# Cross attention of a two-block transformer in pairs of heads: narrower query weight tiles and a new order of its steps among the matrix tiles

## What is computed

```python
def memory_cross_attention(h, mem_n, wq, wk, wv, wo):     # X_HEADS = 4, X_HEAD_DIM = 128
    q = (h @ wq).reshape(b, s, X_HEADS, X_HEAD_DIM)        # 256x2048 @ 2048x512
    k = (mem_n @ wk).reshape(b, m, X_HEADS, X_HEAD_DIM)
    v = (mem_n @ wv).reshape(b, m, X_HEADS, X_HEAD_DIM)
    sc = jnp.einsum('bshd,bmhd->bhsm', q, k).astype(jnp.float32) * (X_HEAD_DIM ** -0.5)
    p = jax.nn.softmax(sc, axis=-1).astype(v.dtype)
    o = jnp.einsum('bhsm,bmhd->bshd', p, v).reshape(b, s, X_HEADS * X_HEAD_DIM)
    return o @ wo                                          # 256x512 @ 512x2048
# in the second block:
x = x + memory_cross_attention(rmsnorm_2(x, g_cross), rmsnorm_2(mem, g_mem), w_q, w_k, w_v, w_o)
x = x + jnp.square(jax.nn.relu(rmsnorm_2(x, g_mlp) @ w_up)) @ w_down
```

## Time and profile before

| | |
|---|---|
| median of 3 runs | 2493.46 us (2493.45 to 2493.95) |
| the profiled execution's own time | 2496.79 us |
| its span in the trace | 2495.5 us |
| TensorE busy (matmul) | 2407.8 us, 96% |
| VectorE busy | 1633.0 us, 65% |
| ScalarE busy | 1211.3 us, 49% |
| 16 DMA engines, queue of the weights | 64.9%, 526.71 MB |
| mean granted TensorE clock | 0.986 |

### The profile page before, as it was taken

The page is one execution under the profiler, slowest core; times in us unless marked ns, Lnnn a source line. Parts: engine busy times, 40 slices in busy tenths (PEclk is TensorE's granted clock), DMA queues, the critical chain, the costliest instruction groups (busy, mean ns, idle before and its releaser), DMA issues.

```text
span 2495.5 us, 28680 instructions
## 1 busy us (share of the span) xinstructions
PE 2407.8 (96%) x11199; PEld 2004.5 (80%) x11199; DVE 1633.0 (65%) x1838; ACT 1211.3 (49%) x1684; POOL 67.7 (3%) x112
## 2 busy tenths in 40 slices
PE   5989999989999999999999999998999999999998
PEld 4777778868888888888878888887788888888886
DVE  7989798678885665755666674554644444555654
ACT  4445556444434444455545555544544444555554
POOL 3000110000000000000000000000000000000000
PEclk8999999999999999999999999999999999999999
DMA  9998886767875666566657554453566666655553
GB/s 336 387 380 293 300 288 240 262 242 274 280 265 176 185 195 189 178 203 192 194 155 201 157 161 131 156 178 109 172 185 185 185 188 188 201 192 196 192 195 114
DMA packets 222359, 530.26 MB, mean 212 GB/s; under 512 B 18778, under 2 KB 23264, under 8 KB 221584
## 3 DMA queue, kind: packets, MB, share of 16 engines
q1 hardware_dynamic: 221280, 526.71, 64.9%
q0 software_dynamic: 640, 0.63, 0.2%
q10 hardware_dynamic: 304, 1.09, 0.1%
HBM read 526.26 MB, written 2.10 MB: 212 GB/s over the span
## 4 chain that ended last, share of the span: by engine, by line
PE 85%; DVE 7%; DMA 3%; issue 2%; ACT 2%; POOL 1%; DVEq 0%; ACTq 0%; POOLq 0%
PE ps L617 26%; PE ps L619 26%; PE ps L618 26%; PE ps L613 2%; DVE ada_acc L1583 1%; DVE wlo L1569 1%; DMA raw<-in_w_in 1%; PE ps L740 1%; DVE silu_gate L1924 1%; PE ps L763 1%; DVE ada_acc L1596 1%; ACT whi L1135 1%; DMA raw<-in_w_v_cross 1%; PE ps L687 1%; DMA raw<-in_w_k_cross 1%
## 5 line engine op out<-in xcount | busy, mean ns | idle before, releaser
L1135 ACT ACTIVATE whi<-raw 128x1024 fp32r<-128x1024 f32 (+2 forms) x804 | 848.2, 1056 | 1155.4 <-PE ps L619 1070.1
L1569 DVE TENSOR_TENSOR wlo<-raw,whi 128x1024 fp32r<-128x1024 f32 (+2 forms) x804 | 974.0, 1216 | 454.4 <-ACT whi L1135 452.4
L617 PE MATMUL ps<-whi,h_hi 128*128 128x512 f32 (+1 forms) x2080 | 825.7, 397 | 12.4 <-DVE h_lo L1644 5.6
L619 PE MATMUL ps<-wlo,h_hi 128*128 128x512 f32 (+1 forms) x2080 | 813.7, 391 | 0.0
L618 PE MATMUL ps<-whi,h_lo 128*128 128x512 f32 (+1 forms) x2080 | 812.9, 391 | 0.0
L617 PEld LDWEIGHTS ps<-whi,h_hi 128*128 128x128 f32 x2080 | 394.0, 189 | 96.2 <-DVE h_lo L1644 6.5
L619 PEld LDWEIGHTS ps<-wlo,h_hi 128*128 128x128 f32 x2080 | 393.2, 189 | 82.4
L618 PEld LDWEIGHTS ps<-whi,h_lo 128*128 128x128 f32 x2080 | 393.9, 189 | 78.3 <-issue 0.7
L617 PE MATMUL ps<-whi,src_hi 128*128 128x512 f32 x864 | 336.3, 389 | 0.0
L619 PE MATMUL ps<-wlo,src_hi 128*128 128x512 f32 x864 | 336.1, 389 | 0.0
L618 PE MATMUL ps<-whi,src_lo 128*128 128x512 f32 x864 | 336.1, 389 | 0.0
(11 more groups left out here) (285 smaller groups left out, 1600.0 us busy)
## 6 DMA issues: line engine op xcount, KB each, us to landing
raw<-in_w_up SPq DMA_DIRECT2D x216, 512.0 KB, 3.8
raw<-in_w_down SPq DMA_DIRECT2D x216, 512.0 KB, 4.4
raw<-in_w_ada SPq DMA_DIRECT2D x192, 512.0 KB, 6.0
raw<-in_w_in SPq DMA_DIRECT2D x168, 512.0 KB, 4.7
raw<-in_w_gate SPq DMA_DIRECT2D x88, 512.0 KB, 3.8
raw<-in_w_out SPq DMA_DIRECT2D x64, 512.0 KB, 4.4
raw<-in_w_k_cross SPq DMA_DIRECT2D x8, 512.0 KB, 9.7
raw<-in_w_v_cross SPq DMA_DIRECT2D x8, 512.0 KB, 8.6
```

Source lines behind the costliest of these rows:

```text
L617: T.matmul(dst, ah, bh, start=first, stop=False)
L619: return T.matmul(dst, ah, bl, start=False, stop=last)
L1135: A.activation(whi[n % SPLIT][:, 0:size], raw[f % RAW][:, 0:size], ACT.Copy).then_inc(*s_hi.next(n))
L1569: V.tensor_tensor(wlo[n % SPLIT][:, 0:size], raw[w_fetch[n] % RAW][:, 0:size], r32(whi[n % SPLIT][:, 0:size]), ALU.subtract).then_inc(*s_l ...
```

## The change

- `w_q_cross_2` is cut into 8 tiles of another shape: four blocks of 128 rows by 256 columns (two heads), still 128x1024. A row of it in HBM is 1 KB, not 2 KB. Their order is `QX_ORDER` = (half, j): half 0 is heads 0 and 1, half 1 heads 2 and 3, j the quarter of the contraction. Half 0 is complete after the fifth tile. `quad_tile` makes 24 products of 256 columns for each. Half 0 accumulates in banks 0 and 1, half 1 in banks 6 and 7.
- The unit X becomes two pairs, X0 (banks 4, 5) and X1 (banks 6, 7, its own buffers `work3`). Each step handles two heads, and one bank for each half of the rows.
- X0's query transposes stand inside tile 5, its scores behind it, its first weight transposes inside tile 7. The rest stands between the last query tile and the output tiles, and X1's steps among the output tiles 0 and 1.
- ScalarE's and VectorE's programs get the pairs' steps between their `ahead` and `low` calls; VectorE's `low(N_OX + 4)` to `low(N_OX + 6)` stand ahead of both `x_add`.

The diff, cut to its core. First the tiles, the buffers and TensorE's program:

```diff
-    N_QX = col_tiles(a["w_q_cross_2"][0], KD, 0)
+    QX_ORDER = [(0, 0), (0, 1), (1, 0), (0, 2), (0, 3), (1, 1), (1, 2), (1, 3)]
+    N_QX = len(weights)
+    for half, j in QX_ORDER:
+        weights.append((a["w_q_cross_2"][0][4 * j * P:(4 * j + 4) * P, half * S:(half + 1) * S].rearrange("(k p) n -> p k n", p=P), BANK))
...
+    CROSS = [dict(name=f"X{g}", g=g, bank=4 + 2 * g, scale=128 ** -0.5, qT=b[0], pT=(b[1], b[0]), sc=b[2:]) for g, b in enumerate((work2, work3))]
...
-                dst = raw[r][:, 0:2 * width].rearrange("p (k n) -> p k n", k=2) if width else raw[r][:, :]
+                dst = raw[r][:, 0:2 * width].rearrange("p (k n) -> p k n", k=src.shape[1]) if width else raw[r][:, :]
...
-        for j in range(8):
-            T.wait_ge(*s_hl.at(H_QX, max(j, 1)))
-            col_tile(N_QX + j, j, KD, 0, h_hi, h_lo)
-            second_blocks(H_QX, j)
-        T.wait_ge(*s_post.at("qx"))
-        for step in range(10):
-            unit_step(U["X"], step)
-        T.wait_ge(*s_ov.at("X", 1))
-        transposes(4, [(k * S + m * P, ox[:, m, k * P:(k + 1) * P]) for k in range(4) for m in range(MT)]).then_inc(*s_oxt.next())
+        def quad_tile(n, half, j, between):
+            T.wait_ge(*s_lo.at(n))
+            wh, wl = whi[n % SPLIT], wlo[n % SPLIT]
+            for kk in range(4):
+                k, c = 4 * j + kk, slice(kk * S, (kk + 1) * S)
+                for m in range(MT):
+                    c_m = slice(m * P, (m + 1) * P)
+                    ins = products(ps[:, 6 * half + m, 0:S], h_hi[:, k, c_m], h_lo[:, k, c_m], wh[:, c], wl[:, c], k == 0, k == KD - 1)
+                if kk == 1 and between:
+                    between()
+            ins.then_inc(*s_mm.next(n))
...
+        for q, (half, j) in enumerate(QX_ORDER):
+            T.wait_ge(*s_hl.at(H_QX, 2 * j + 1))
+            quad_tile(N_QX + q, half, j, {5: lambda: cross_q(CROSS[0]), 7: lambda: cross_p(CROSS[0], 0)}[q] if q in (5, 7) else None)
+            second_blocks(H_QX, q)
+            if q == 5:
+                cross_scores(CROSS[0])
+        cross_p(CROSS[0], 1)
+        cross_pv(CROSS[0], 0)
+        cross_q(CROSS[1])
+        cross_pv(CROSS[0], 1)
+        cross_scores(CROSS[1])
+        cross_o(CROSS[0])
+        T.wait_ge(*s_oxl.at(0))
+        ox_tile(0)
+        for t in range(MT):
+            cross_p(CROSS[1], t)
+        T.wait_ge(*s_lo.at(N_OX + 1))
+        half_tile("cross", N_OX + 1, 0, *ox_parts(1), (0,), False, False)
+        for t in range(MT):
+            cross_pv(CROSS[1], t)
+        half_tile("cross", N_OX + 1, 0, *ox_parts(1), (1,), False, False, (0,))
+        cross_o(CROSS[1])
+        half_tile("cross", N_OX + 1, 0, *ox_parts(1), (1,), False, False, (1,)).then_inc(*s_mm.next(N_OX + 1))
+        T.wait_ge(*s_oxl.at(1))
+        ox_tile(2)
+        ox_tile(3)
```

```diff
+        for q in range(8):
+            if q == 5:
+                cross_post(CROSS[0])
+            if q == 7:
+                cross_exp(CROSS[0], 0)
+            ahead(N_QX + q + (0, 1, 3, 3, 3, 3, 3, 3)[q])
...
+            if q == 5:
+                cross_q(CROSS[0])
+        cross_exp(CROSS[0], 1)
+        cross_p(CROSS[0], 0)
+        cross_post(CROSS[1])
+        cross_p(CROSS[0], 1)
+        cross_q(CROSS[1])
+        ahead(N_OX + 3)
+        cross_o(CROSS[0])
+        cross_exp(CROSS[1], 0)
+        cross_exp(CROSS[1], 1)
+        for t in range(MT):
+            cross_p(CROSS[1], t)
+        ahead(N_OX + 4)
+        cross_o(CROSS[1])
```

```diff
+        for q in range(8):
+            if q == 7:
+                for t in range(MT):
+                    cross_max(CROSS[0], t)
+            low(N_QX + q + (1, 1, 2, 2, 2, 2, 2, 2)[q])
...
+        for t in range(MT):
+            cross_sums(CROSS[0], t)
+        low(N_OX + 2)
+        cross_out(CROSS[0], 0)
+        cross_out(CROSS[0], 1)
+        cross_max(CROSS[1], 0)
+        cross_o(CROSS[0])
+        cross_max(CROSS[1], 1)
+        low(N_OX + 3)
+        for t in range(MT):
+            cross_sums(CROSS[1], t)
+        for t in range(MT):
+            cross_out(CROSS[1], t)
+        cross_o(CROSS[1])
+        low(N_OX + 6)
         for m in range(MT):
             x_add(3, "cross", m, 0, N_OX, 4)
-            low(N_OX + 5 + m)
         low(N_OX + 7)
```

More of the change, by code:

```diff
@@ L633, in col_tile, with half_tile @@
                         between(2 * kk + m)
-        def half_tile(name, n, half, hi, lo, ms, first, last):
+        def half_tile(name, n, half, hi, lo, ms, first, last, columns=(0, 1)):
             wh, wl = whi[n % SPLIT], wlo[n % SPLIT]
             for m in ms:
-                for i in range(2):
+                for i in columns:
                     c, c_m = slice(i * BANK, (i + 1) * BANK), slice(m * P, (m + 1) * P)
@@ new lines, in cross_q, with cross_scores @@
+        def cross_q(u):
+            T.wait_ge(*s_post.at("qx", u["g"]))
+            transposes(u["bank"], [(i * S + m * P, qx[:, m, (2 * u["g"] + i) * P:(2 * u["g"] + i + 1) * P])
+                                   for i in range(2) for m in range(MT)]).then_inc(*s_qkt.next(u["name"], "q"))
+        def cross_scores(u):
+            T.wait_ge(*s_qke.at(u["name"], "done"))
+            for t in range(MT):
+                for i in range(2):
+                    ins = T.matmul(ps[:, u["bank"] + t, i * S:(i + 1) * S], u["qT"][:, i * S + t * P:i * S + (t + 1) * P], kxT[:, 2 * u["g"] + i, :],
+                                   start=True, stop=True)
+                ins.then_inc(*s_sc.next(u["name"], t))
@@ new lines, in cross_p, with cross_pv @@
+        def cross_p(u, t):
+            T.wait_ge(*s_pr.at(u["name"], t))
+            transposes(u["bank"] + t, [((2 * kt + i) * P, u["sc"][t][:, i * S + kt * P:i * S + (kt + 1) * P])
+                                       for kt in range(2) for i in range(2)]).then_inc(*s_pt.next(u["name"], t))
+        def cross_pv(u, t):
+            T.wait_ge(*s_pe.at(u["name"], t))
+            for i in range(2):
+                c = (2 * u["g"] + i) * P
+                for kt in range(2):
+                    ins = T.matmul(ps[:, u["bank"] + t, i * P:(i + 1) * P], u["pT"][t][:, (2 * kt + i) * P:(2 * kt + i + 1) * P], vx[:, kt, c:c + P],
+                                   start=kt == 0, stop=kt == 1)
+            ins.then_inc(*s_o.next(u["name"], t))
@@ L1084, in tensor_program, with cross_o, ox_tile @@
+        def cross_o(u):
+            T.wait_ge(*s_ov.at(u["name"], 1))
+            transposes(u["bank"], [(i * S + m * P, ox[:, m, (2 * u["g"] + i) * P:(2 * u["g"] + i + 1) * P])
+                                   for i in range(2) for m in range(MT)]).then_inc(*s_oxt.next(u["g"]))
         ox_parts = lambda c: (ox_hi[:, c % 4, :], ox_lo[:, c % 4, :])
-        for c in range(4):
-            if c % 2 == 0:
-                T.wait_ge(*s_oxl.at(c // 2))
+        def ox_tile(c):
             T.wait_ge(*s_lo.at(N_OX + c))
@@ L1489, in scalar_program @@
                 h_group(H_QX, (c - 22) // 2, X_BANKS[H_QX], g_cross, None)
[L1492 to L1501, removed]
@@ L1502, in scalar_program, with cross_post, cross_q @@
-        A.wait_ge(*s_oxt.at())
-        for b in range(2):
-            A.activation(ox_hi[:, 2 * b:2 * b + 2, :].rearrange("p k n -> p (k n)"), ps[:, 4 + b, :], ACT.Copy).then_inc(*s_oxh.next(b))
+        def cross_post(u):
+            A.wait_ge(*s_mm.at(N_QX + (4, 7)[u["g"]]))
+            c0 = 2 * u["g"] * P
+            scaled_post(6 * u["g"], qx[:, :, c0:c0 + 2 * P], 2 * P, "cross", "qx", u["g"])
+        def cross_q(u):
+            A.wait_ge(*s_qkt.at(u["name"], "q"))
+            A.activation(u["qT"][:, 0:2 * S], ps[:, u["bank"], :], ACT.Copy).then_inc(*s_qke.next(u["name"], "done"))
@@ new lines, in cross_exp, with cross_p @@
+        def cross_exp(u, t):
+            A.wait_ge(*s_ng.at(u["name"], t))
+            for i in range(2):
+                sc, c = u["sc"][t][:, i * S:(i + 1) * S], 2 * t + i
+                ins = A.activation(sc, sc, ACT.Exp, bias=nm[u["g"]][:, c:c + 1], scale=u["scale"], accum_out=den[u["g"]][:, c:c + 1])
+            ins.then_inc(*s_ex.next(u["name"], t))
+        def cross_p(u, t):
+            A.wait_ge(*s_pt.at(u["name"], t))
+            A.activation(u["pT"][t][:, 0:4 * P], ps[:, u["bank"] + t, :], ACT.Copy).then_inc(*s_pe.next(u["name"], t))
@@ L2058, in vector_program @@
         x_add(2, "mix", 1, 1, N_WO2, KD)
[L2059 to L2068, removed]
@@ L2069, in vector_program, with cross_max, cross_sums @@
-        low(N_OX + 4)
+        def cross_max(u, t):
+            sc, c = u["sc"][t][:, 0:2 * S], nm[u["g"]][:, 2 * t:2 * t + 2]
+            V.wait_ge(*s_sc.at(u["name"], t))
+            own(V.tensor_copy(sc, ps[:, u["bank"] + t, :]))
+            own(V.tensor_reduce(c, sc.rearrange("p (u n) -> p u n", u=2), AX, ALU.max))
+            V.tensor_scalar(c, c, -u["scale"], None, ALU.mult).then_inc(*s_ng.next(u["name"], t))
+        def cross_sums(u, t):
+            V.wait_ge(*s_ex.at(u["name"], t))
```

(11 more changed lines are left out.)

16 lines of the change are left out of this document (10 added, 6 removed).

## The result

The changed kernel takes 2481.83 us (median of 5 runs, 2479.50 to 2482.03) against 2493.46 us for the kernel before (5 runs, 2491.93 to 2496.70): a ratio of 0.9950, interval 0.9939 to 0.9960, so 11.6 us less. A second set, beside three of the experiments (e5 to e7), gave 2480.05 (5 runs) against 2494.01 (11 runs), ratio 0.9947, interval 0.9935 to 0.9960, 14.0 us less. 12.8 us less were forecast, and 2480.7 us as the time.

A forecast was written before the change was run, and what follows sets the result against it. TensorE, busy 96% of the span, was taken as the bound, losing time in the cross attention. Stage terms summed to 55.1 us against 67.9; 12.8 less gave 2484.0, and the median 3.33 lower 2480.7 us; range 2478.4 to 2484.4.

The forecast's parts named there:

- The sum: TensorE's cross stage, first query product to transposes behind the output tiles: 55.1 us against 67.9, 12.8 less.
- Query tiles: TensorE, 192 products of 256 columns at 0.120 us: 23.0 us against 21.8 before, so 1.3 more.
- the bounds 0.107 and 0.179: Lower and upper limits in us for a 256-column product: two steps of 0.053, and a weight load's duration.
- Float32 instructions: TensorE's attention: 0.22 us per 256-column instruction, 0.11 per 128-column one or transpose; 10.6 us in all.
- Expected waits: TensorE waits 1.5 us for X0's high and low output parts, then 0.8 for X1's; 2.3 in all.
- the restarts: TensorE after a switch or wait: about 14 at 0.1 us or a little less, 1.1 us.
- Tile 5's transposes: X0's query copies end near 1714.2, TensorE asks at 1714.5: covered by half of tile 5.
- D: VectorE's half-width steps cost nearly the full-width 1.23 us; 3.6 us lost, 2484.3 us; chance 0.06.
- A: Clock falls once more between last scores and tile N_OX; costs 1.7 to 3.4 us, 2482.4 to 2484.1; chance 0.13.
- B: Weight loads surface: a 256-column query product costs 0.179 us, 11.3 us more, 2492.0 us; chance 0.03.
- C: Query products cost 0.227 us whatever their width, 20.5 us more than in the sum, 2501.2 us; chance 0.03.
- The missing waits on `low`: TensorE among output tiles: `low` parts ready before asked for, so 2.3 us of waits and restarts go.

The follow-up runs named there:

- e5: e4 with the earlier wide query tiles (2 blocks by 512 columns) and both pairs' queries copied after tile 7; 2486.29 us.
- e7: Changed kernel plus one unused 1.15 us VectorE addition between `low(N_OX + 3)` and X1's reciprocals; 2481.57 us.
- e2: Kernel before with only the new VectorE order of `low` and additions; 2491.30 us, ratio 0.9988.
- e1: Changed kernel with VectorE's earlier order of `low` and additions at the end of the cross stage; 2482.94 us.
- e3: Kernel before with filler products, results unused, in TensorE's waits of unit X; 2490.96 us, ratio 0.9989.
- e4: Changed kernel with all X0 steps behind the last query tile and X1's a step behind it; 2484.14 us.

## Why the prediction was right

**The sum** held at nearly every term. Query tiles: 0.120 us a product, as taken; the bounds 0.107 and 0.179 were not needed. Float32 instructions: eight scores in 1.89 us, as in the earlier trace rows. Expected waits 1.5 and 0.8, measured 1.41 and 0.72, both on the low part of the output. The stage was forecast at 55.1 us and took 54.46. The 0.6 us between are small surcharges in the sum: the waits were 0.2 too long, and the restarts, taken at 1.1 us, are left with 0.7 once all else is put in as measured. The execution before that the sum was made against had two falls of the clock; with one, as in e2's unit X, its stage would be 1.27 us shorter, so the stage gains 12.2 to 13.5 us. The medians, 11.6 and 14.0 us less, lie on both sides of that; that the forecast total came within 1.2 us of both is luck in part, since the first query product alone moves by 4.4 us between executions.

**Each forecast step.** Tile 5's transposes found X0's queries ready, since ScalarE's copies began in time. The timeline of ScalarE after shows them at 1711.92 to 1712.96, where TensorE asked at 1713.16:

```profile
1711.92 1.04 ACT L1258 ACTIVATE cross_q<-ps,root_mean_square 128x256 f32<-128x256 f32 x2 [0.72 <-PE ps L620]
```

That is 0.2 us to spare, less than the 0.3 forecast. VectorE's half-width steps took 0.69 us each (against D's 1.23), and X1's last maxima and its reciprocals were done just as TensorE asked; the timeline of VectorE after:

```profile
1729.97 0.69 DVE L2162 TENSOR_REDUCE neg_max<-w_s 128x2 f32<-128x512 f32 x1
1730.69 0.17 DVE L2163 TENSOR_SCALAR neg_max<-neg_max 128x2 f32<-128x2 f32 x1
1730.77 1.22 DVE L1668 TENSOR_TENSOR wlo<-raw,whi 128x1024 fp32r<-128x1024 f32 x1
1731.91 0.28 DVE L2167 RECIPROCAL reciprocal<-denominator 128x2 f32<-128x2 f32 x2
```

The reciprocals end at 1732.19, and the transposes start at 1732.26 with no wait; e7 shows that one more step there costs 1.07 us of its 1.1. The DMAs of the 1 KB rows landed in 3.6 us (3.4 before): covered.

**Where the 13.47 us come from**: by the experiments 2.35 the order of `low` and additions (e1) and 4.16 the clock (e3); by the count of products (192 x 0.120 against 96 x 0.227) minus 1.3 for the narrow tiles. What is left, 13.47 - 2.35 - 4.16 + 1.3 = 8.3, is cover: 3.56 of it by X0's steps inside the query tiles (e4), the rest by the pairs beside each other and beside the output tiles. That rest, some 4.7, is a difference, not an experiment of its own, and the parts could overlap a little: e3 and e1 were measured on different kernels, and the clock's 4.16 would be 2.9 against e2.

**Rivals.** A didn't come in the changed kernel, but it is real: e5 paid 1.6 us for it, just under the 1.7 that the prediction put as its lower price, after a stretch only 0.7 us longer than the changed kernel's and shorter than the 3.5 and 4.7 us that the prediction set against it. By that comparison of stretches the risk looked smaller than e5 shows it. The rule of the Trainium skill named beside it ("TensorE: Matmul & The Clock Gate", section "PE-mode transpose") agrees with e5's fall as with the earlier trace rows; e4, with the same transposes and waits and no fall, shows that it doesn't settle the matter. B and C fell with the 0.12 us between products. The 2.5 ns of the Trainium skill (same page, section "Back-to-back issue gap", which gives them for a single matmul by itself) in the place of the 13 beyond columns / 2.4 GHz don't hold for this stream: 256 / 2.4 GHz = 107 ns, and 120 were measured. D fell with 0.69 us for a half-width step. The missing waits on `low` came out as the sum had them.

## What to carry to other kernels

Where one engine is the bound and a stage is a chain over three engines, lay the programs side by side with durations from the trace and look where that engine asks before the others have answered; the distances so found held to 0.6 us in 55. Splitting the chain's data in two pays where the halves cover each other; a costlier tile shape pays only if it lets the chain start under work that is there anyway. Judge a change of a few microseconds by distances inside the trace, which repeated to 0.05 us here where the clock stayed up, and not by totals that spread over 2.5 to 6.6. Look at the granted clock in the same stretch first: one fall more or less moved such a distance by 1.3 to 1.6 us.

## What the runs showed that was not expected

- The clock falls of the unit X differ between executions: the profiled execution before had two (3.4 and 6.8 us), e2's, whose unit X is the same, one of 6.8, and its stage was 1.27 us shorter for it.
- e4 and e5 have the same stretch of 2.6 us of transposes and waits; one execution kept its clock, the other lost it for 3.4 us. What decides was not tried.
- The first query product, 1.7 ms into the span behind unchanged code, stood anywhere from 1692.5 to 1696.9 in ten profiles, and the later it stood, the longer, by and large, the clock had been at half ahead of it (13.6 us in the three earliest, 30.6 in the two latest). What makes the clock fall there more often in one execution than in another stays open.
